# Three RMS norms of a two-block transformer kernel: squares added in pairs on GpSimd, half as many sums on TensorE

## The reference

```python
def _rmsnorm(x, gain, eps=NORM_EPS):
    x32 = x.astype(jnp.float32)
    y = x32 * lax.rsqrt(jnp.mean(x32 * x32, axis=-1, keepdims=True) + eps)
    return (y * gain).astype(x.dtype)

for l in range(DEPTH):                        # DEPTH = 2
    h = _rmsnorm(x, norm_mix[l])              # l = 0: untouched, l = 1: changed ("mix1")
    p = h @ w_in[l]                           # then the four branches
    x = x + merged @ w_out[l]
    h = _rmsnorm(x, norm_ffn[l])              # l = 0: changed ("dense"), l = 1: untouched
    if l % 2 == 0:
        x = x + _swiglu(h, ffn_w1[l // 2], ffn_w3[l // 2], ffn_w2[l // 2])
    else:
        x = x + _moe_ffn(h, router[l // 2], moe_w1[l // 2], moe_w3[l // 2], moe_w2[l // 2])
h = rms_norm(x, norm_gain)                    # changed ("second")
proj = h @ w_in_2
```

## Time and profile before

| | |
|---|---|
| median of 3 runs | 1524.29 us (1523.73 to 1526.12) |
| the profiled execution | 1525.84 us, of which its span is 1524.1 us |
| PE busy | 1487.8 us (98%) |
| DVE busy | 1096.2 us (72%) |
| ACT busy | 857.0 us (56%) |
| POOL busy | 116.2 us (8%) |
| DMA | 292.97 MB, mean 192 GB/s |

### The profile page before, as it was taken

One profiled execution on the slowest core, in us unless ns is written; L12 is line 12 of the kernel. 1 busy time (PEld: TensorE's weight loads), 2 busy tenths in 40 slices (PEclk: granted clock), 3 DMA queues, 4 the chain that ended last, 5 costly groups with the idle time before them and its releaser, 6 DMA issues. The chain is left out here.

```text
span 1524.1 us, 24774 instructions
## 1 busy us (share of the span) xinstructions
PE 1487.8 (98%) x9870; PEld 1299.1 (85%) x9870; DVE 1096.2 (72%) x1555; ACT 857.0 (56%) x1192; POOL 116.2 (8%) x128
## 2 busy tenths in 40 slices
PE   8999999999999999899999799999999999999999
PEld 7889999899999998899999777777777778797788
DVE  5888654756555678967457788898888987766644
ACT  4776435354444466743542667777777774566422
POOL 1057000000000002620000200000000000000000
PEclk9999999999999999999999799999999999999999
DMA  8532233345555454223325189999999997632222
GB/s 325 173 117 98 83 119 103 117 161 183 190 181 199 157 174 155 85 82 110 112 98 199 54 313 353 354 364 354 352 353 356 364 355 228 213 120 84 84 92 75
DMA packets 83398, 292.97 MB, mean 192 GB/s; under 512 B 9159, under 2 KB 12991, under 8 KB 83023
## 3 DMA queue, kind: packets, MB, share of 16 engines
q1 hardware_dynamic: 83279, 291.34, 54.3%
HBM read 290.22 MB, written 1.08 MB: 191 GB/s over the span
## 5 line engine op out<-in xcount | busy, mean ns | idle before, releaser
L394 DVE TENSOR_TENSOR ring_lo<-ring,weights_hi 128x1024 fp32r<-128x1024 f32 x343 | 418.1, 1233 | 175.9 <-ACT weights_hi L373 172.6
L373 ACT ACTIVATE weights_hi<-ring 128x1024 fp32r<-128x1024 f32 x343 | 355.6, 1055 | 201.9 <-PE bank_P L275 162.3
L273 PE MATMUL bank_P<-h_hi,weights_hi 128*128 128x256 f32 x1456 | 425.4, 292 | 11.3 <-DVE ring_lo L394 7.9
L275 PE MATMUL bank_P<-h_hi,ring_lo 128*128 128x256 f32 x1456 | 412.6, 283 | 0.0
L274 PE MATMUL bank_P<-h_lo,weights_hi 128*128 128x256 f32 x1456 | 411.4, 283 | 0.0
L273 PEld LDWEIGHTS bank_P<-h_hi,weights_hi 128*128 128x128 f32 x1456 | 276.3, 190 | 23.0 <-issue 8.4
L275 PEld LDWEIGHTS bank_P<-h_hi,ring_lo 128*128 128x128 f32 x1456 | 280.8, 193 | 0.0
L274 PEld LDWEIGHTS bank_P<-h_lo,weights_hi 128*128 128x128 f32 x1456 | 276.9, 190 | 1.7 <-issue 1.4
L274 PE MATMUL bank_P<-ring_lo,gathered_hi 128*96 128x512 f32 (+1 forms) x384 | 144.0, 375 | 0.0
L530 POOL TENSOR_TENSOR arena<-arena 128x256 f32<-128x256 f32 x98 | 91.3, 932 | 361.8 <-ACT arena L1027 345.5
L394 DVE TENSOR_TENSOR ring_lo<-ring,tokens_hi 128x1024 fp32r<-128x1024 f32 x76 | 90.4, 1217 | 0.1
(11 more groups left out here) (527 smaller groups left out, 2797.0 us busy)
## 6 DMA issues: line engine op xcount, KB each, us to landing
ring<-stream SPq DMA_DIRECT2D x541, 512.0 KB, 4.7
cst<-consts SPq DMA_DIRECT2D x1, 1712.0 KB, 16.9
arena<-params SPq DMA_DIRECT2D x1, 1211.0 KB, 6.0
arena<-x SPq DMA_DIRECT2D x2, 512.0 KB, 4.3
arena<-bias_vec SPq DMA_DIRECT2D x8, 128.0 KB, 3.2
out<-arena SPq DMA_DIRECT2D x3, 256.0 KB, 2.1
arena<-params SPq DMA_DIRECT2D x2, 256.0 KB, 11.1
arena<-bias_vec SPq DMA_DIRECT2D x8, 64.0 KB, 2.7
```

The costliest lines, as they stand in the source:

```text
L273: pe.matmul(out, hi, x_hi, start=start, stop=False, skip_group_check=True)
L275: return pe.matmul(out, lo, x_hi, start=False, stop=stop, skip_group_check=True)
L373: a.activation(self.slots[i % len(self.slots)], env["ring"][:, slot, :], ACT.Copy)\
L394: v.tensor_tensor(env["ring_lo"][:, slot, :], env["ring"][:, slot, :], self.slots[i % len(self.slots)].bitcast(F32), ALU.subtract).then_in ...
```

## The change

In three norms (dense, mix1, second) GpSimd adds the two squared tiles of each pair in place, as soon as ScalarE has squared them (`pair_sums`), and TensorE multiplies the four sums by ones instead of the eight squares (`paired`). The sum of pair q - 1 is issued before steps 2, 4 and 6 of the first block, and that of the last pair before step 0 of the second block (`last_squares`), so that `ssx` comes one block later. On GpSimd the adds stand at the end of mix0 for dense, and ahead of the memsets in mix1 and in second. Layer 0's mixer norm stays as it was.

```diff
+def pair_sums(g, squares, arrived, summed):
+    for q in range(KD // 2):
+        g.wait_ge(*arrived(q))
+        g.tensor_tensor(squares[:, 2 * q, :], squares[:, 2 * q, :], squares[:, 2 * q + 1, :], ALU.add).then_inc(*summed(q))
...
     def gpsimd(g):                                                    # mix0 and mix1
         if layer:
             g.wait_ge(*after("h2_lo_3", "mix0"))
+            pair_sums(g, sqx, lambda q: after(f"sqx_{q}"), lambda q: done("pool", f"sq_pair_{q}"))
         g.memset(praw[:, :, 0:1], 0.0).then_inc(*done("pool", "praw_zeroed"))
...
+        if layer == 0:
+            pair_sums(g, sqx2, lambda q: after(f"sqx2_{q}"), lambda q: done("pool", f"sq2_pair_{q}"))
...
-                return blocks.unsplit(bank[:, j * T:(j + 1) * T], xg, None if blocks.n else square_sum)
+                ahead = {0: square_sum, 1: last_squares if layer else None}.get(blocks.n)
+                return blocks.unsplit(bank[:, j * T:(j + 1) * T], xg, ahead)
...
         def square_sum(q):                                            # mix0 and mix1
-            for p in ([q], [0], [1, 2, 3], [], [])[1 + q if layer else 0]:
-                pe.wait_ge(*after(f"sqx_{p}"))
-                for k in (2 * p, 2 * p + 1):
+            if layer and q:
+                paired(q - 1)
+            if not layer:
+                pe.wait_ge(*after(f"sqx_{q}"))
+                for k in (2 * q, 2 * q + 1):
                     mm = pe.matmul(Z1[:, 0:T], C("ones"), sqx[:, k, :], start=(k == 0), stop=(k == KD - 1))
-                if p == 3:
+                if q == 3:
                     mm.then_inc(*done("pe", "ssx"))
             pe.wait_ge(*after(f"xg_{q}"))
+
+        def paired(p):
+            pe.wait_ge(*after(f"sq_pair_{p}"))
+            mm = pe.matmul(Z1[:, 0:T], C("ones"), sqx[:, 2 * p, :], start=(p == 0), stop=(p == 3))
+            if p == 3:
+                mm.then_inc(*done("pe", "ssx"))
+
+        def last_squares(q):
+            if q == 0:
+                paired(3)
...
         def square_sum(q):                                            # dense
-            pe.wait_ge(*after(f"sqx2_{q}", "mix0"))
-            for k in (2 * q, 2 * q + 1):
-                mm = pe.matmul(banks["Z1"][:, 0:T], env["C"]("ones"), squares[:, k, :], start=(k == 0), stop=(k == KD - 1))
-                if k == 0:
-                    env["mix0_blocks"].release(mm)
-            if q == 3:
+            if q:
+                paired(q - 1)
+            pe.wait_ge(*after(f"xg2_{q}", "mix0"))
+
+        def paired(p):
+            pe.wait_ge(*after(f"sq2_pair_{p}", "mix0"))
+            mm = pe.matmul(banks["Z1"][:, 0:T], env["C"]("ones"), squares[:, 2 * p, :], start=(p == 0), stop=(p == 3))
+            if p == 0:
+                env["mix0_blocks"].release(mm)
+            if p == 3:
                 mm.then_inc(*done("pe", "ssx2"))
-            pe.wait_ge(*after(f"xg2_{q}", "mix0"))
...
     def gpsimd(g):                                                    # second
+        pair_sums(g, sqx, lambda q: after(f"sqx_{q}"), lambda q: done("pool", f"sq_pair_{q}"))
         g.wait_ge(*after("x_3", "moe"))
...
         def square_sum(q):                                            # second
-            for p in ([0], [1, 2, 3], [], [])[q]:
-                pe.wait_ge(*after(f"sqx_{p}"))
-                for k in (2 * p, 2 * p + 1):
-                    mm = pe.matmul(BX[:, 0:T], C("ones"), sqx[:, k, :], start=(k == 0), stop=(k == KD - 1))
-                if p == 3:
-                    mm.then_inc(*done("pe", "ssx"))
+            if q:
+                paired(q - 1)
             pe.wait_ge(*after(f"xg_{q}"))
```

More of the change, by code:

```diff
@@ L1969, in up @@
                 if blocks.n < RAW:
-                    mm = blocks.unsplit(bank[:, i * T:(i + 1) * T], xg, None if blocks.n else square_sum)
+                    mm = blocks.unsplit(bank[:, i * T:(i + 1) * T], xg, {0: square_sum, 1: last_squares}.get(blocks.n))
                     continue
@@ L2288, in square_sum, with paired, last_squares @@
         def square_sum(q):
-            for p in ([0], [1, 2, 3], [], [])[q]:
-                pe.wait_ge(*after(f"sqx_{p}"))
-                for k in (2 * p, 2 * p + 1):
-                    mm = pe.matmul(BX[:, 0:T], C("ones"), sqx[:, k, :], start=(k == 0), stop=(k == KD - 1))
-                if p == 3:
-                    mm.then_inc(*done("pe", "ssx"))
-            pe.wait_ge(*after(f"xg_{q}"))
+            if q:
+                paired(q - 1)
+            pe.wait_ge(*after(f"xg_{q}"))
+        def paired(p):
+            pe.wait_ge(*after(f"sq_pair_{p}"))
+            mm = pe.matmul(BX[:, 0:T], C("ones"), sqx[:, 2 * p, :], start=(p == 0), stop=(p == 3))
+            if p == 3:
+                mm.then_inc(*done("pe", "ssx"))
+        def last_squares(q):
+            if q == 0:
+                paired(3)
         def tile(bank, j, waits=None):
             if blocks.n < RAW:
-                return blocks.unsplit(bank[:, j * T:(j + 1) * T], xg, None if blocks.n else square_sum)
+                return blocks.unsplit(bank[:, j * T:(j + 1) * T], xg, {0: square_sum, 1: last_squares}.get(blocks.n))
             hi, lo = blocks.split()
```

## The result

| | before | changed |
|---|---|---|
| median of 9 runs each | 1524.29 us (1522.87 to 1526.48) | 1529.17 us (1526.19 to 1531.34) |
| the profiled execution | 1525.84 us, span 1524.1 | 1529.96 us, span 1528.2 |
| PE busy | 1487.8 us | 1488.2 us |
| DVE busy | 1096.2 us | 1103.5 us |

The ratio is 1.0028, with a 95% interval of 1.0018 to 1.0037: 4.3 us slower (2.7 to 5.6). The forecast was 1524.9, with a range up to 1527.2.

What follows compares the result with a forecast made beforehand. TensorE, busy 98% of the span, bounds the kernel, but VectorE bounds the start of second. Dense -1.1, mix1 -1.0, second +1.0 and half clock +1.7 give +0.6 us: 1524.9 against the median, range 1521.2 to 1527.2.

Steps and rivals of the forecast that it cites:

- the last sentence on mix1: In mix1, GpSimd's memsets moved behind the adds end by about 528; what waits for them comes behind 537.
- The later `xg` are wanted 1.3 us apart and keep up: In mix1 and second, TensorE waits for none of VectorE's normed tiles after `xg_1`.
- the upper bound of `xg_1`: In mix1, TensorE waits 1.0 us for `xg_1` if both `tensor_scalar` take 0.83 us; 0.55 was taken.
- Mix1: Norm of mix1: 1.7 us saved, less 0.15 for a later start and 0.55 for `xg_1`, gains 1.0 us.
- Dense: Norm of dense: sum 0.86 us earlier plus slack 0.25 gains 1.1 us, with a TensorE wait of 0.6.
- The adds: Twelve GpSimd adds over three norms, median 0.74 us each; no wait on the adds themselves.
- rival 3: GpSimd's adds take up to 1.75 us, sums wait in second and mix1: +2.5 or +4.2 us; chance 0.09.
- Second: Start of second: VectorE's chain from the reciprocal comes 1.0 us later, so second loses 1.0; TensorE waits 2.7 us.
- The half clock behind it: After the 2.7 us wait in second, 3.4 us at 1.2 GHz instead of 2.4 is likely: +1.7 us.
- Rival 4: Gains ahead of the experts are lost in them: 2.1 us vanish, +2.7 us stays, 1527.0; chance 0.05.
- Rival 2: All 12 removed products are saved, second's norm having slack as in mix1: -5.1 us, 1519.2; chance 0.03.
- the slower side: Whole kernel above 1527.34 us, 0.2% over before: chance 0.14, against 0.11 for faster and 0.75 for no change.

Runs made afterwards that it cites:

- dense only: The changed kernel with mix1's and second's edits undone, so only the norm of dense is changed: 1524.56 us, ratio 0.9992 to the kernel before.
- memsets first: The changed kernel with mix1's three memsets ahead of GpSimd's adds: 1523.16 us, ratio 0.9990; with second's norm also undone 1522.44 us, ratio 0.9986.
- second only: The kernel before with only the norm of second changed: 1525.81 us, ratio 1.0006 to the kernel before.

## Why the prediction was wrong

**The step that failed** is the last sentence on mix1: "GpSimd's memsets, now behind the adds, end by about 528; what waits for them comes in the mixer". The time was right (they ended at 526.3), but I asked only who waits for the zeros by a semaphore, and not whose instructions the memset holds up while it runs. With it fell the sentence "The later `xg` are wanted 1.3 us apart and keep up": `xg_2` came 3.00 us late. I had weighed that very lock for the adds, 0.28 to 0.83 us for a `tensor_scalar`, and taken the upper bound of `xg_1` from it. The moved memset is nearly five times as long as an add, and no bound of mix1 held it. Mix1 was forecast at -1.0 us, bounds -1.6 to -0.5. It came out at +4.3 to the fifth block: without the memset it is -0.7, and the memset adds 5.0, of which 3.0 are the wait and most of the rest is the half clock behind it (1.7). The -0.7 is less than the -1.0 forecast because the waits cost a little more than the terms for them: `xg_1` was set at 0.55, and its product starts 1.18 us behind the sum's, where 0.43 would do: 0.75. The upper end of my range for the kernel was missed by 2.0 us for this term alone.

**Dense** was right, in part by an offset that I had not seen: forecast -1.1, measured -1.2 in the trace and, alone, by ratio. The square root came at 333.11 in a frame that is 0.23 later, so 332.9 as forecast; the wait was 0.29 us instead of 0.6. The memset is gone from there and no longer slows a cast of VectorE in the chain, here before and after:

```profile
346.50 0.50 DVE L2036 CAST hidden_hi<-arena 128x256 fp32r<-128x256 f32 x1
```

```profile
345.85 0.29 DVE L2066 CAST hidden_hi<-arena 128x256 fp32r<-128x256 f32 x1
```

With the memset back in its place (dense only, memsets first) dense takes 192.20 us and TensorE's wait is 0.50, without it 191.99 and 0.29. I had left this collision out too; without its going dense gains 1.0.

**The adds** were right: TensorE's wait for `xg_1` was 0.59 us (0.55 forecast), and no product with ones waited for an add (rival 3). They took 0.73 to 0.77 us each.

**Second** was right in its chain: forecast +1.0, measured +1.1, with a wait of 2.63 us (2.7). The half clock behind it was forecast as likely and fell in four of six profiled kernels; the times say less: second only cost +0.9 us, not 2.7. It belongs in the sum with its chance.

**The rivals.** Rival 4 falls: it expects nothing of dense and mix1, and with the memsets first these two bring 2.1 us (0.9 to 3.5). Rival 2 falls by VectorE's chain. The time went to the slower side (0.14 in my chances) for none of the reasons that I had listed there, but by the mechanism that I had weighed for the adds, one instruction further on.

## What to carry to other kernels

When a queue's work is moved, ask of each instruction in it not only who waits for its result but what else runs beside it at its new time. A memset on GpSimd is idle work until it falls on VectorE's `tensor_scalar`. And a product taken off TensorE also takes away cover: the collision cost 0.15 us with six products with ones in front of it and a start 1.6 us sooner, and 5.0 us without either.

## What the runs showed of the hardware

A `tensor_scalar` of VectorE (128x256, float32) that meets GpSimd waits for its whole instruction, a memset (write only) included: 3.70 us beside a memset of 3.59, where six take 1.67 undisturbed. Memsets that stand back to back let none through (4.42 us with halves of 1.80), while a wait of GpSimd on a semaphore between them lets one through (1.97). Between the adds, each with a semaphore wait ahead of it, one passed each time (0.77 and 0.81 us). A cast (128x256) that met the end of the memset took 0.50 us instead of 0.29. A `tensor_tensor` with two SBUF inputs was not slowed by a memset (1.21 us). What in GpSimd's issue decides this was not tried further.
